# Hybrid-attention transformer block on one core: a longer opening with three ring slots, and a shorter last gate round

## What is computed

```python
mod = silu(c) @ w_ada + b_ada                       # 6 x 2048: shift1, scale1, gate1, ...
h = rms_norm(x, norm1_w) * (1 + scale1) + shift1
proj = h @ w_in                                     # q_a k_a v_a q_f k_f v_f f_logit g_a g_f
y_a = swa_sink_attention(rope(norm(q_a)), rope(norm(k_a)), v_a) @ w_o_swa   # 8 heads of 128
y_f = forgetting_attention(norm(q_f), norm(k_f), v_f, logsigmoid(f_logit)) @ w_o_fox
x = x + gate1 * ((sigmoid(g_a) * y_a + sigmoid(g_f) * y_f) @ w_out)
h2 = rms_norm(x, norm2_w) * (1 + scale2) + shift2
g, u = split(h2 @ w_ffn_in);  x = x + gate2 * ((silu(g) * u) @ w_ffn_out)
```

## Time and profile before

| | us |
|---|---|
| runs, median of 3 | 2676.62 (2676.03 to 2676.74) |
| profiled execution | 2676.34 |
| its span (core 0), mean granted clock on PE | 2674.7, 0.989 |
| PE, DVE, ACT, POOL busy | 2627.8, 1996.8, 1042.5, 311.0 |
| opening 0 to 144.5: PE, DVE, ACT busy | 113.5, 114.0, 58.2 |
| phase A, 144.5 to 510: PE busy | 359.2 |
| phase B, 510 to 957.8: PE busy | 446.7 |

### The profile page before, as it was taken

The page is one execution under the profiler, slowest core; times in us unless marked ns, Lnnn a source line. Parts: engine busy times, 40 slices in busy tenths (PEclk is TensorE's granted clock), DMA queues, the critical chain, the costliest instruction groups (busy, mean ns, idle before and its releaser), DMA issues.

```text
span 2674.7 us, 44661 instructions
## 1 busy us (share of the span) xinstructions
PE 2627.8 (98%) x17066; PEld 2394.5 (90%) x17066; DVE 1996.8 (75%) x3101; ACT 1042.5 (39%) x1420; POOL 311.0 (12%) x290
## 2 busy tenths in 40 slices
...
GB/s 335 319 174 205 189 204 193 145 109 95 103 96 101 78 231 236 235 233 234 148 94 157 161 137 157 164 136 154 166 138 151 166 206 341 166 348 181 261 219 119
DMA packets 399677, 487.18 MB, mean 182 GB/s; under 512 B 19220, under 2 KB 338984, under 8 KB 398984
## 3 DMA queue, kind: packets, MB, share of 16 engines
...
q0 software_dynamic: 32896, 127.28, 13.5%
...
HBM read 414.80 MB, written 69.73 MB: 181 GB/s over the span
## 4 chain that ended last, share of the span: by engine, by line
PE 91%; DVE 3%; DMA 2%; issue 2%; ACT 1%; SPq 1%; DVEq 0%; ACTq 0%
PE bank L924 15%; PE bank L927 15%; PE bank L926 15%; PE bank L601 12%; PE bank L603 12%; PE bank L602 12%; DMA ramp_w<-in_w_ada 2%; PE bank L753 1%; DVE ramp_acc L1386 1%; PE bank L779 1%; SPq L502 1%; DVE ada_acc L1338 1%; PE bank L742 1%; PE bank L873 1%; PE bank L875 1%
## 5 line engine op out<-in xcount | busy, mean ns | idle before, releaser
L924 PE MATMUL bank<-mov,w_slot 128*128 128x256 f32 x3472 | 980.3, 282 | 1.1 <-ACT blocks L1229 1.1
L927 PE MATMUL bank<-mov,w_slot 128*128 128x256 f32 x3472 | 978.8, 282 | 0.0
L926 PE MATMUL bank<-mov,w_slot 128*128 128x256 f32 x3472 | 978.6, 282 | 0.0
L924 PEld LDWEIGHTS bank<-mov,w_slot 128*128 128x128 f32 x3472 | 661.6, 191 | 1.4 <-ACT blocks L1229 1.3
L926 PEld LDWEIGHTS bank<-mov,w_slot 128*128 128x128 f32 x3472 | 662.1, 191 | 0.0
L927 PEld LDWEIGHTS bank<-mov,w_slot 128*128 128x128 f32 x3472 | 661.6, 191 | 0.0
L601 PE MATMUL bank<-h_hi,w_hi 128*128 128x512 f32 x1280 | 506.2, 395 | 0.0
L603 PE MATMUL bank<-h_hi,w_lo 128*128 128x512 f32 x1280 | 500.0, 391 | 0.0
L602 PE MATMUL bank<-h_lo,w_hi 128*128 128x512 f32 x1280 | 499.0, 390 | 0.0
L1317 DVE TENSOR_TENSOR w_lo<-w_raw,w_hi 128x1024 fp32r<-128x1024 f32 x192 | 245.2, 1278 | 325.7 <-ACT w_hi L954 325.1
L1168 ACT ACTIVATE w_slot<-w_raw 128x768 fp32r<-128x768 f32 x248 | 209.6, 845 | 542.9 <-PE bank L927 538.3
...
...
## 6 DMA issues: line engine op xcount, KB each, us to landing
...
w_raw<-in_w_ada SPq DMA_DIRECT2D x128, 512.0 KB
...
mov<-u_fm POOLq DMA_DIRECT2D x22, 1792.0 KB, 22.1
...
w_raw<-in_w_in SPq DMA_DIRECT2D x128, 256.0 KB
...
```

What stands on the lines that cost most here:

```text
L924: nc.tensor.matmul(dst, lhsT=wh, rhs=xh, start=s == 0 and t == 0, stop=False, skip_group_check=True)
L926: nc.tensor.matmul(dst, lhsT=wh, rhs=xl, start=False, stop=False, skip_group_check=True)
L927: mm = nc.tensor.matmul(dst, lhsT=wl, rhs=xh, start=False, stop=last, skip_group_check=True)
```

## The change

1. **The last gate pair in the opening.** `first_unit` has two more column tiles: the g_f columns of i = 7. It has 21 matmuls per tile, in banks 2 and 3 first. `load_first` brings 768 KB in two DMAs, and the parts have 1536 columns in three places, `g_first`, `g_hi0`/`g_lo0`, `g_hi1`/`g_lo1`. ACT takes the sigmoid of the two banks at the end of the opening and stores them from its own queue. The last head pair of B has four gate units (`B_LAST`) in place of eight. Its window attention's tail moves behind the units j = 0 and j = 1 of merge step 0, and C multiplies `of` before `oa`.
2. **All normalised tiles at once.** PE forms the 16 tiles ahead of everything else of the opening, ACT copies each to memory on the chip (`xn`), and `h_tile` reads it there. `fill` puts 8 matmuls without use behind it. DVE makes the diagonals ahead of the first step of the sums.
3. **A ring of three.** The quarters, now called chunks, use three slots (`R_SLOTS`), chunk n waits for the sums over chunk n - 3, and the w_in columns are put between chunks by a table (`first_behind`).
4. **Smaller ones.** Two DMAs and two ACT copies take the place of DVE's memsets of `fq_rows` and `fk_rows`. In phase A's first head `x_low` stands before the split of j = 4.

```diff
--- before.py
+++ after.py
+RG = (2,) * G_N
+RG0 = tuple(range(0, KD, 2))
+R_SLOTS = 3
+GW = 6 * P
...
+B_LAST = 4
+C_R, C_N, C_I = B_R + B_N * (B_I - 1) + B_LAST, 4, D // UN
...
+        xn = at("xn", H + KD * T, KD * S)
+        g_raw = [at("g_raw0", STORE + 17 * T, GK * GW), at("g_raw1", STORE + 14 * T, GK * GW)]
+        g_hi = [at("g_hi0", STORE + 8 * T, GK * GW, F32R), at("g_hi1", STORE + 2 * T, GK * GW, F32R)]
+        g_lo = [at("g_lo0", STORE + 11 * T, GK * GW, F32R), at("g_lo1", STORE + 5 * T, GK * GW, F32R)]
+        g_first = [at("g_first_hi", H + 10 * T, GK * GW, F32R), at("g_first_lo", H + 13 * T, GK * GW, F32R)]
...
-                sp.dma_start(g_raw[:, (p % 2) * GK * 4 * P:(p % 2 + 1) * GK * 4 * P].rearrange("p (k n) -> p k n", k=GK),
-                             w_in_k[:, k0:k0 + GK, KA0:KA0 + 4 * P]).then_inc(g_landed[p % 2], 16)
...
+                for c0, a, b in ((KA0, 0, 4 * P), (G0 + D + (B_I - 1) * UN, 4 * P, GW)):
+                    sp.dma_start(dst[:, :, a:b], w_in_k[:, k0:k0 + GK, c0:c0 + b - a]).then_inc(g_landed[p % 2], 16)
...
+            def load_chunk(c):
+                p, j = divmod(c, STEP)
+                w = RG[p] * P
+                for b, c0 in enumerate((D, 0)):
+                    sp.dma_start(chunk(c)[:, b], w_ada_k[:, j * UK:(j + 1) * UK, c0 + RG0[p] * P:c0 + RG0[p] * P + w]
+                                 ).then_inc(chunk_landed[c % R_SLOTS], 16)
...
-            for j in range(STEP):
-                load_quarter(0, j)
-            load_first(0)
-            for p in range(1, G_N):
-                for j in range(STEP):
...
+            first_behind = {2: 0, 8: 1, 10: 2, 13: 3, 17: 4, 21: 5, 25: 6, 29: 7}
+            for n in range(STEP * len(RG)):
+                if n >= R_SLOTS:
+                    sp.wait_ge(ada_mac, macs_to(n - R_SLOTS))
+                load_chunk(n)
+                if n in first_behind:
+                    p = first_behind[n]
+                    if p == 1:
+                        sp.wait_ge(xn_ready, KD)
+                    if p >= 2:
+                        split(p - 2)
+                    load_first(p)
+
+            sp.wait_ge(ada_mac, macs_to(STEP * len(RG) - 2))
...
+            with sp.Fori(0, B_I - 1) as i:
+                load_gates(i, B_N)
+            load_gates(B_I - 1, B_LAST)
...
-                    w = (w_oa_k, w_of_k)[j // 2]
+                    w = (w_of_k, w_oa_k)[j // 2]
...
+            def normalised(k):
+
+                if k >= len(NORM_BANKS):
+                    pe.wait_ge(xn_copied, k - len(NORM_BANKS) + 1)
+                for tb in range(TB):
+                    mm = nc.tensor.matmul(bank[NORM_BANKS[k % len(NORM_BANKS)]][:, tb * P:(tb + 1) * P],
+                                          lhsT=x_rows[:, tb * D + k * P:tb * D + (k + 1) * P],
+                                          rhs=diag[:, tb * P:(tb + 1) * P], start=True, stop=True)
+                mm.then_inc(xn_ready, 1)
...
-                for t, b in ((0, 6), (2, 7), (None, 5), (1, 0), (3, 1)):
+                for t, b in ((4, 2), (5, 3), (0, 6), (2, 7), (None, 5), (1, 0), (3, 1)):
...
-            normalised(0)
-            for p in range(G_N):
-                ramp_cols(p)
-                if p:
-                    first_unit(p - 1, 1)
-                else:
-                    pe.wait_ge(fl_ready, 1)
-                first_unit(p, 0)
-                if p < G_N - 1:
...
+            for k in range(KD):
+                normalised(k)
+            ramp_cols(0)
+            pe.wait_ge(xn_copied, KD)
+            fill(7, 8)
+            pe.wait_ge(fl_ready, 1)
+            for k in range(KD):
+                first_unit(k)
+                if k in COLS_BEHIND:
+                    ramp_cols(COLS_BEHIND[k])
...
+                        if i == 0:
+                            pe.wait_ge(gate_out, 2)
...
-                for j in range(B_N):
+                for j in range(B_N if h < B_I - 1 else B_LAST):
...
                         pe.wait_ge(m_step, 6 * i + 4)
-                    hi, lo = ((oa_hi, oa_lo), (of_hi, of_lo))[j // 2]
+                    if i == 0 and j != 2:
+                        pe.wait_ge(o_ready, (2 * HQ, 2 * HQ + 1, None, 2 * HQ + 2)[j])
+                    hi, lo = ((of_hi, of_lo), (oa_hi, oa_lo))[j // 2]
                     gemm(C_R + C_N * i + j, C_R + j, hi, lo, UK * (j % 2),
...
-                    if j == 2:
+                    if i == 0 and j == 0:
+                        probabilities(swa_pt, 2 * HQ)
+                    if i == 0 and j == 1:
+                        weighted_values(swa_blocks, 2 * HQ)
+                    if j == (3 if i == 0 else 2):
...
+            def copy_norm(k):
+                act.wait_ge(xn_ready, k + 1)
+                nc.scalar.activation(tile(xn, k), bank[NORM_BANKS[k % len(NORM_BANKS)]][:], ACT.Copy).then_inc(xn_copied, 1)
+
...
+            for k in range(KD - 2):
+                copy_norm(k)
             act.wait_ge(fl_landed, 16)
             nc.scalar.activation(fl_hi[:], fl_raw[:], ACT.Copy).then_inc(fl_hi_done, 1)
...
-                act.wait_ge(g_landed[p % 2], 16 * (p // 2 + 1))
-                if p >= 2:
-                    act.wait_ge(unit_done, p - 1)
...
+                    act.wait_ge(xn_copied, KD)
+                    act.wait_ge(scale_ready, half // GK + 1)
...
+            act.dma_start(fq_set[:], consts[:, ROWS0:ROWS0 + S]).then_inc(tab_landed, 16)
+            act.dma_start(fk_set[:], consts[:, ROWS0 + S:ROWS0 + 2 * S]).then_inc(tab_landed, 16)
...
+            act.wait_ge(gate_done, 1)
+            for t in range(2):
+                nc.scalar.activation(tile(rot, A_I + t), bank[2 + t][:], ACT.Sigmoid).then_inc(gate_out, 1)
...
             split(ph_a, 0, 1 - LEAD, False)
+            act.wait_ge(gate_out, 2)
+            act.dma_start(gate_fm[KD + 2 * (B_I - 1):KD + 2 * B_I].rearrange("k p s -> p k s"),
+                          rot[:, A_I * S:(A_I + 2) * S].rearrange("p (k s) -> p k s", k=2)).then_inc(gate_early, 16)
...
+            nc.scalar.activation(fq_rows[:], fq_set[:], ACT.Copy)
+            nc.scalar.activation(fk_rows[:], fk_set[:], ACT.Copy).then_inc(f_dve, 1)
...
+                        swa_turned(h)
+                if last:
+                    act.wait_ge(unit_done, B_R + B_N * h + B_LAST)
+                    gate(2, 0, last_gates)
+                    high_output(tile(of_hi, h), 2 * h + 1)
+                    exponentials(swa_blocks, 2 * h + 2, h)
+                    return
...
             v.tensor_copy(ones_r[:], ones[:])
-            v.memset(fq_rows[:].bitcast(F32), 0.0)
-            v.memset(fk_rows[:].bitcast(F32), 0.0).then_inc(rows_zeroed, 1)
-            dve.wait_ge(rows_zeroed, 1)
-            for r0 in (64, 96):
-                v.memset(fq_rows[r0:r0 + HQ, :].bitcast(F32), 1.0)
-            v.memset(fk_rows[32:32 + HQ, :].bitcast(F32), 1.0).then_inc(f_dve, 1)
...
-            for p in range(G_N):
+            def diagonals():
...
+                for tb in range(TB):
+                    v.tensor_scalar(diag[:, tb * P:(tb + 1) * P], ident[:], rr[:, tb:tb + 1], None,
+                                    ALU.mult).then_inc(diag_ready, 1)
...
+            h_behind = {(k // 2 + 1, 8 + 2 * (k % 2)): k for k in range(KD - 2)}
+            w_behind = {(1, 1): 0} | {(p, 12): p for p in range(1, G_N)}
...
+                    if (p, m) == (0, 0):
+                        diagonals()
...
-                    if p == 1 and m == 1:
-                        dve.wait_ge(fl_hi_done, 1)
-                        v.tensor_tensor(fl_lo[:], fl_raw[:], fl_hi[:].bitcast(F32), ALU.subtract).then_inc(fl_ready, 1)
-                        first_low(0)
-                    if p and m in (8, 10):
-                        h_low(2 * (p - 1) + (0 if m == 8 else 1))
-                    if p and m == 12:
-                        first_low(p)
...
                 for j in range(A_N):
+                    if first and j == 4:
+                        x_low(i)
                     split(ph_a, i, j, last)
                     if j == 1:
                         y_norm(i + 1)
-                    if j == 4:
+                    if not first and j == 4:
                         x_low(i)
...
-                for j in range(B_N):
+                for j in range(B_LAST if last else B_N):
+                    if last and j == 1:
+                        masked(fox_blocks, fox_at, foxmask, 2 * h + 1, 8 * h + 4)
                     split(ph_b, h, j, last)
-                    if j == 1:
...
+                if last:
+                    low_output(tile(of_lo, h), tile(of_hi, h), 2 * h + 1)
+                    masked(swa_blocks, swa_at, swamask, 2 * h + 2, 8 * h + 8, h)
+                    normalise(swa_blocks, 2 * h + 2, h)
+                    return
                 low_output(tile(oa_lo, h), tile(oa_hi, h), 2 * h + 2)
```

(15 more changed lines are left out.)

272 lines of the change are left out of this document (151 added, 121 removed).

## The result

| us | before | after |
|---|---|---|
| median of 20 runs each, on the same chip | 2675.93 | 2679.97 |
| ratio, 95% interval | | 1.0014 (1.0008 to 1.0020) |
| span of the profiled execution | 2674.7 | 2677.9 |
| first of the last opening columns | 130.45 | 149.98 |
| first matmul behind the opening (the first head's norm) | 144.62 | 168.17 |

The change is 4.0 us slower, 0.14%: inside what counts as no change, but with an interval that lies above 1. I had forecast a gain of 4.6, so the sign is wrong, though 2679.97 lies inside the range of 2664 to 2681 that I gave. The table splits the 3.2 us between the spans by marks on PE: +19.5 up to the last sums, +4.0 for the tail of the opening, +2.3 in phase A, 0.0 in the head pairs between, -22.6 from the last head pair on.

A forecast was written before the change was run, and what follows sets the result against it. Loads bound the opening and PE the rest, but for single waits; -22.1 + 15.0 + 4.1 - 1.8 = -4.8 on 2676.62 gave 2671.8, say 2672.0 us, range 2664 to 2681.

The forecast's parts named there:

- Last head pair and merge: End of the kernel: four gate units fewer and one wait gone, less later probabilities, -22.1 us.
- Bytes: Opening: each w_in load grows from 0.52 to 0.79 MB, +6.0 us at 353 GB/s.
- Two dry spells: Start of the opening: the load queue runs empty for 4.3 and 3.9 us; with the bytes +15.0.
- From there on the queue stays full: Opening after the second dry spell: no more gaps, groups of 14.3 us, last columns at 145.4.
- rival B: Opening: three slots too few throughout, each of seven groups goes dry; 2684.4 us if refills come 2.5 later; chance 0.09.
- Tail: End of the opening: 63 matmuls behind the last columns, before 45, nothing hidden, +4.1 us.
- First head: Phase A's first head: sq_low 2.8 us earlier, less about 1.0 for a table reload, -1.8 (0 to -2.8).
- The first wait: Phase A's first head: PE's 5.51 us wait for sq_low, whose result was to come 2.8 us earlier.
- the reload: ACT's table reload after the sigmoid, ahead of phase A's first root: about +1.0 us in the sq_low chain.
- The sum: Whole kernel: -22.1 + 15.0 + 4.1 - 1.8 = -4.8 us, a gain too small to be called faster.

The follow-up runs named there:

- e1: Changed kernel with a fourth ring slot for the w_ada chunks in the same memory, nothing else: 2668.26 us, ratio 0.9967 to the kernel before.
- e8: Changed kernel with four ring slots and without the last gate pair's product in the opening (output lacks those gates): 2656.66 us, ratio 0.9930 to the kernel before.
- e7: Changed kernel with a plain copy in place of the last gate pair's sigmoid, so no ACT table reload: 2678.90 us, ratio 1.0012 to the kernel before.
- e6: Changed kernel with four slots, ACT's high parts early, second w_in load behind chunk 7, x_low early in all phase A heads: 2664.23 us, ratio 0.9956 to before.
- e2: Changed kernel, three slots, ACT's high parts ahead of tile copies, second w_in load behind chunk 6: 2674.10 us, ratio 0.9993 to the kernel before.

## Why the prediction was wrong, point by point

- **Last head pair and merge, -22.1.** Right: -22.6. The forgetting probabilities came 0.17 later than the shift of all else, and the wait of 1.08 in the earlier trace rows is gone:

```profile
948.02 1.20 PE L798 MATMUL bank<-small_all,logits 128*128 128x128 f32 x9
...
964.15 0.98 PE L798 MATMUL bank<-small_all,logits 128*128 128x128 f32 x7
```

- **Bytes, +6.0.** Right: 6.4 (e1 against e8), to the 2 us that one profile tells.
- **Two dry spells, 4.3 and 3.9 us.** Right in place and cause: 40 to 42 and 54 to 58, DVE standing for ACT's high parts. They were 2.6 and 4.7 us long, so that the sum came out nearer than either. PE's clock rose at 25.5 and not at 27.3, so the tiles were done sooner. Chunk 10 flowed from 58.1, where I had 59.5.
- **"From there on the queue stays full".** This is the step that failed: the refill of a slot in every later group. From chunk 10's first packets to the last columns I had 85.9 us (59.5 to 145.4); it took 91.9, 1.1 us more in each of 5.5 groups. These 6.0 us, less the 1.4 by which chunk 10 was early, are what the columns came late. That is rival B, which I gave 0.09 and priced at a refill of 5.3 us with 0.7 to spare. One refill, from the trace after (windows, then SP):

```profile
82.00:83.50 1.50, 1.50 (x8) 1.21 (x8) 1.50 (x4) 0.00 (x0) 0.00 (x0) 1.00 1.10 362
...
84.00:85.00 1.00, 1.00 (x6) 0.73 (x5) 1.00 (x3) 0.00 (x0) 0.00 (x0) 1.00 0.28 94
...
85.00:85.50 0.50, 0.50 (x4) 0.19 (x3) 0.50 (x1) 0.00 (x0) 0.00 (x0) 1.00 0.50 92
...
85.50:86.00 0.50, 0.50 (x4) 0.42 (x3) 0.50 (x1) 0.00 (x0) 0.00 (x0) 1.00 0.90 246
...
143.00:144.00 1.00, 0.93 (x4) 0.83 (x5) 1.00 (x2) 0.33 (x1) 0.00 (x0) 1.00 0.39 135
...
144.00:146.00 2.00, 2.00 (x11) 1.52 (x10) 2.00 (x4) 0.00 (x0) 0.00 (x0) 1.00 0.00 0
...
84.07 0.92 SPq L545 DMA_DIRECT2D ramp_w<-in_w_ada  x2
```

  The queue runs out about 84.2. The last two chunks of 2.97 us must then have begun at 78.2, so chunk 14's last byte was in by then (worked out, not seen), and DVE started on it at 80.09: 1.9 us, where I had 0.4 at the start and nothing in this sum. Four sums and two low parts took 3.9 (I had 4.2), SP issued at 84.07, and the queue was at its rate again from about 85.5: 1.4 (I had 1.1). Together 7.2 us against 6.0 queued, so 1.2 dry, which is the 1.1 per group. At the end, where the last chunk's bytes ran out about 143.4, chunk 30 was in at 140.4 and DVE started at 141.57: 1.2 us. e1 shows the sign and size: with one chunk more queued the spells are gone. The split is read off one refill, its first part also off the end of the opening. By the Trainium skill, page "DMA: Bandwidth & Descriptors", section "Anatomy of one DMA — SWDGE (gpsimd) path", most of a DMA's fixed 2.0 us is the receipt of the last byte. The page has this for another path than SP's, and the two ends measured here, 1.2 to 1.9 and 1.4, add to 2.6 to 3.3, so the trace gives more; I had weighed it for the two early spells and not for every refill.
- **Tail, +4.1.** Right: +4.0.
- **First head, -1.8.** The first wait went as predicted (5.51 to 3.77) and the reload too (e7, 0.95). What failed is that I stopped at the first wait: DVE, not PE, set the time of the second head's squares, and all that the move gave was given back there (85.10 from the norm, 85.13 with the move undone, 84.48 before). A as a whole is 2.3 longer, 4.1 us off; 1.7 of that is a low stretch of the clock that four other traces of the same phase A don't have, so the step itself was off by about 2.4.
- **The sum.** 4.6 us from the columns (145.4 against 149.98) and 4.1 from phase A, less 0.6 from the tail and the last head pair, are the 8.0 between -4.8 and the span's +3.2.
- **The expectation of e6** was 12 to 14 and it gave 11.6; that of e2 was right in time (2.5, measured 2.1) while its groups weren't.
